# Attention scores as full-array fp32r matmuls on stacked key parts, and the turn of the older mix between the two score products

## The reference, cut to what matters

```python
def diff_attention(q, k, v, q_pos, k_pos, lam):
    s = jnp.einsum("bqhcd,bkhcd->bhcqk", q, k, preferred_element_type=jnp.float32) * (HEAD_DIM ** -0.5)
    mask = k_pos[None, :] <= q_pos[:, None]
    s = jnp.where(mask, s, NEG)
    p = jax.nn.softmax(s, axis=-1)
    w = p[:, :, 0] - lam * p[:, :, 1]
    return jnp.einsum("bhqk,bkhe->bqhe", w.astype(v.dtype), v)
```

## Time and profile before

| | us |
|---|---|
| median of three runs | 2425.14 |
| lowest and highest run | 2422.55, 2428.04 |
| span of the profiled execution | 2420.9 |
| PE busy in the span | 2349.3 (97%) |
| DVE, ACT and POOL busy | 1508.1, 750.4, 843.5 |

### The profile page before, as it was taken

One profiled execution on the slowest core, in us unless ns is written; L12 is line 12 of the kernel. 1 busy time (PEld: TensorE's weight loads), 2 busy tenths in 40 slices (PEclk: granted clock), 3 DMA queues, 4 the chain that ended last, 5 costly groups with the idle time before them and its releaser, 6 DMA issues.

```text
span 2420.9 us, 40635 instructions
## 1 busy us (share of the span) xinstructions
PE 2349.3 (97%) x16326; PEld 2276.2 (94%) x16326; DVE 1508.1 (62%) x2499; ACT 750.4 (31%) x1440; POOL 843.5 (35%) x557
## 2 busy tenths in 40 slices
PE   7899999999999999999999999999999999999998
PEld 6889999999999999999999766699999999999997
DVE  9993257555555576775534577756755555557766
ACT  4452134333333211031100377843433333320103
POOL 0003325544445443332332000043555444443431
PEclk9899999999999999999999999999999999999999
DMA  3155101222222422212256454210222222242212
GB/s 123 38 141 175 53 18 66 82 70 73 71 79 79 166 85 90 88 53 88 88 184 209 126 145 141 71 36 18 70 79 79 79 79 71 70 157 105 79 62 71
DMA packets 107540, 221.41 MB, mean 91 GB/s; under 512 B 35802, under 2 KB 59866, under 8 KB 107362
## 3 DMA queue, kind: packets, MB, share of 16 engines
q1 hardware_dynamic: 94130, 179.95, 23.3%
q10 hardware_dynamic: 13232, 38.94, 4.4%
HBM read 171.79 MB, written 44.71 MB: 89 GB/s over the span
## 4 chain that ended last, share of the span: by engine, by line
PE 84%; DVE 11%; issue 2%; ACT 1%; DMA 1%; POOL 0%; SPq 0%; DVEq 0%; ACTq 0%; POOLq 0%
PE pair L2130 45%; PE pair L2384 12%; PE pair L2387 12%; PE pair L2388 12%; PE pair L2617 1%; DVE nmx L1933 1%; DVE act_lo L1454 1%; DVE Vp L1373 1%; DMA zn<-zblk 1%; DVE wmix L2010 1%; DVE acc L1373 1%; DVE Vp L1795 1%; PE pair L2298 1%; DVE act_lo L1407 0%; DVE G_im L1373 0%
## 5 line engine op out<-in xcount | busy, mean ns | idle before, releaser
L2384 PE MATMUL pair<-act_hi,w_hi 128*128 128x344 f32 x1408 | 450.0, 320 | 6.7 <-DVE gate L1373 3.0
L2388 PE MATMUL pair<-act_hi,w_lo 128*128 128x344 f32 x1408 | 450.1, 320 | 0.0
L2387 PE MATMUL pair<-act_lo,w_hi 128*128 128x344 f32 x1408 | 449.9, 320 | 0.0
L2130 PE MATMUL pair<-act_hi,w_hi 128*128 128x344 f32 x1152 | 371.1, 322 | 2.7 <-DVE act_lo L1373 2.1
L2130 PE MATMUL pair<-act_hi,w_lo 128*128 128x344 f32 x1152 | 368.2, 320 | 0.0
L2130 PE MATMUL pair<-act_lo,w_hi 128*128 128x344 f32 x1152 | 368.0, 319 | 0.0
L732 POOL CAST w_hi<-w_raw 128x1024 fp32r<-128x1024 f32 x90 | 114.8, 1276 | 722.8 <-issue 309.5
L1373 DVE TENSOR_TENSOR X<-X,pair 128x344 f32<-128x344 f32 x528 | 252.9, 507 | 150.8 <-PE pair L2130 150.8
L2130 PE MATMUL pair<-hid_hi,w_hi 128*128 128x344 f32 x1056 | 338.2, 320 | 1.1 <-POOL w_lo L735 1.1
L2130 PE MATMUL pair<-hid_lo,w_hi 128*128 128x344 f32 x1056 | 338.5, 321 | 0.0
L2130 PE MATMUL pair<-hid_hi,w_lo 128*128 128x344 f32 x1056 | 338.0, 320 | 0.0
(11 more groups left out here) (308 smaller groups left out, 4199.7 us busy)
## 6 DMA issues: line engine op xcount, KB each, us to landing
w_raw<-w SPq DMA_DIRECT2D x180, 512.0 KB, 4.0
hid_raw<-hid SPq DMA_DIRECT2D x20, 1032.0 KB, 5.7
hid<-gate ACTq DMA_DIRECT2D x22, 516.0 KB, 2.7
hid<-gate_odd ACTq DMA_DIRECT2D x22, 516.0 KB, 2.6
kpg<-cache_k SPq DMA_DIRECT2D x16, 512.0 KB, 5.4
vpg<-cache_v SPq DMA_DIRECT2D x16, 512.0 KB, 7.0
qd<-qt SPq DMA_DIRECT2D x28, 256.0 KB, 5.4
ublk<-x_b SPq DMA_DIRECT2D x8, 576.0 KB, 8.3
```

Source lines behind the costliest of these rows:

```text
L2130: return t_.matmul(out, lhsT, rhs, start=start, stop=stop)
L2384: ins = t_.matmul(out, wh, rhs[k][0], start=first and k == 0, stop=False, skip_group_check=True)
L2387: t_.matmul(out, wh, rhs[k][1], start=False, stop=False, skip_group_check=True)
L2388: last = t_.matmul(out, wl, rhs[k][0], start=False, stop=k == HK - 1, skip_group_check=True)
```

## The change

It has six parts.

1. **Scores.** The key tile `kh` of a component has the high parts of its 64 dimensions on partitions 0 to 63 and the low parts on 64 to 127. The queries' high parts lie twice, in `qh`, and their low parts twice, in `ql0` or `ql1`. One component's scores are then two fp32r matmuls over 128 rows for each 512 columns or rest of them, high and low, and one mask matmul of 128 columns. Columns are in plain order; the maximum and the exponential read them so.
2. **Order on PE.** T(v-1) stands between S(v+1, 0) and S(v+1, 1), no longer behind both.
3. **Splitting 16 rows of queries and keys** in the projection stage: ACT copies 1024 columns into the high part (`high_of_rows`), POOL subtracts (`low_of_rows`), ACT stores both parts to the new HBM scratch `qk` (`store_split`). There are two high buffers and one low buffer, so each low row waits for the two stores of the row ahead of it. The store to `qt` is gone.
4. **Where POOL does it**: behind the weight split of pair 3 four rows, and behind those of pairs 4 to 9 two rows each. DVE's eviction into a slot of `stage` waits for the low row that is read from it.
5. **Loads of a head**: 13 transfers and 3.5 MB (4 of keys, 8 of queries, each 256 KB, and the values) in place of 9 and 2 MB. Those of head 1's keys move behind the last eviction of the projections.
6. Semaphores of `X` and of the last output are merged, and the scratch of POOL's descriptors is set to 1024 bytes.

```diff
+SPLIT_ORDER = (2, 3, 0, 1) + tuple(range(4, 2 * KT))
...
             def load_queries(h, par, into=None):
...
+                for c in range(2):
+                    for l, out in enumerate((high[:, 1 - c, :], low[1 - c])):
+                        for g in range(2):
+                            sp.dma_start(out[64 * g:64 * g + 64, :].bitcast(F32), d["qk"][0, l, 2 * h + c].rearrange("m j t -> (m j) t")
+                                         ).then_inc(hd_in[par], 16)
...
+            def low_of_rows(i):
+
+                pool.wait_ge(hl_hi, i + 1)
+                if i:
+                    pool.wait_ge(hl_out, 32 * i)
+                g.tensor_tensor(hq[:, 2, :], rows_in_turn(i), hq[:, i % 2, :].bitcast(F32), ALU.subtract).then_inc(hl_lo, 1)
...
+            for u in range(U_KVQ - 2, SEG1, 2):
+                split_one(u, 1)
+                split_one(u + 1, 1)
+                for i in {3: (0, 1, 2, 3), 4: (4, 5), 5: (6, 7), 6: (8, 9), 7: (10, 11), 8: (12, 13), 9: (14, 15)}.get((u - U_KVQ) // 2, ()):
+                    low_of_rows(i)
...
+            def store_split(i):
+
+                tt = SPLIT_ORDER[i]
+                act.wait_ge(hl_lo, i + 1)
+                for l, x in enumerate((i % 2, 2)):
+                    act.dma_start(rows_of(d["qk"][tt // KT, l])[tt % KT], hq[:, x, :].bitcast(F32)).then_inc(hl_out, 16)
+
+            def high_of_rows(i):
+
+                if i >= 2:
+                    act.wait_ge(hl_out, 32 * (i - 1))
+                a.activation(hq[:, i % 2, :], rows_in_turn(i), ACT.Copy).then_inc(hl_hi, 1)
+                if i:
+                    store_split(i - 1)
...
             def scores(v, x):
...
-                w = (i + 1) * 64
-                for g in range(2):
-                    rows = slice(64 * g, 64 * g + 64)
-                    mm(bank[2 * x + g][:, 0:w], (qd[par] if h else qd_first)[rows, x, i * P:(i + 1) * P], kh[rows, par, x, 0:w], True, False)
-                for g in range(2):
-                    rows = slice(64 * g, 64 * g + 64)
-                    last = mm(bank[2 * x + g][:, w - 64:w], identb[rows, :], maskb[rows, :], False, True)
-                last.then_inc(a_s, 1)
+                q = slice(i * P, (i + 1) * P)
+                high = (qh[par] if h else qh_first)[:, x, q]
+                low = ql1[x][:, q] if par else ql0[:, x, q]
+                for k0 in range(0, (i + 1) * P, SEQ // 2):
+                    ks = slice(k0, min(k0 + SEQ // 2, (i + 1) * P))
+                    final = ks.stop < (i + 1) * P
+                    mm(pair[x][:, ks], high, kh[par][:, x, ks], True, False)
+                    mm(pair[x][:, ks], low, kh[par][:, x, ks], False, final)
+                mm(pair[x][:, q], identb[:], maskb[:], False, True).then_inc(a_s, 1)
...
                 if v + 1 < NH * KT:
                     scores(v + 1, 0)
-                    scores(v + 1, 1)
                 if v >= 1:
                     turn(v - 1)
+                if v + 1 < NH * KT:
+                    scores(v + 1, 1)
```

More of the change, by code:

```diff
@@ L140, in build @@
         identb = place("identb", [P, P], BF16)
-        maskb = place("maskb", [P, 64], BF16)
+        maskb = place("maskb", [P, P], BF16)
         ones = place("ones", [P, P], F32)
@@ L158, in build @@
         ngain = place("ngain", [P, 2, KT], F32)
+        HQ_AT = top[0]
+        hq = place("hq", [P, 3, SEQ], F32R)
         STMP_AT = top[0]
@@ L317, in build @@
         blk_in = sem("blk_in")
-        x_in = [sem(f"x_in{n}") for n in range(NC)]
+        x_in = sem("x_in")
         w_in = [sem(f"w_in{r}") for r in range(4)]
@@ L1904, in _ @@
             c.step(v_.tensor_scalar(ngain[:], gains[:, 2:4, :], -1.0, None, ALU.mult))
-            for n in range(NC):
-                dve.wait_ge(x_in[n], 16)
+            dve.wait_ge(x_in, 16 * NC)
             with dve.Fori(0, KT - 2) as m:
@@ L1941, in _ @@
                     dve.wait_ge(d_smp, kvq_tile - 2)
+                    if kvq_tile - 3 < 2 * KT and not slots[kvq_tile - 3][1]:
+                        dve.wait_ge(hl_lo, SPLIT_ORDER.index(kvq_tile - 3) + 1)
                     for x in range(2):
@@ L1956, in _ @@
                 slot = slots[kvq_tile][0]
-                if not slots[kvq_tile][1]:
+                if kvq_tile >= KT and not slots[kvq_tile][1]:
                     seen[slot] += 16
@@ L2763, in constants @@
     tok = order[:P]
[L2764 to L2774 removed]
+    masked = np.where(tok[None, :] > tok[:, None], f(-1e30), f(0))
     nvec = np.concatenate([np.arange(NW), L * np.arange(NJ), L * NJ * np.arange(NI)]).astype(f)
```

114 lines of the change are left out of this document (56 added, 58 removed).

## The result

The changed kernel takes 2470.7 us (median of 4 runs, 2466.1 to 2474.4); the kernel before takes 2425.0. The ratio is 1.019, with a 95% interval of 1.0177 to 1.0203. The direction was forecast; the size was not: +45.7 us in place of +14.3, and outside the range of 2427 to 2453.

What follows compares the result with a forecast made beforehand. PE, busy 97% of the span, was taken as the bound. Attention +12.8 and projections +1.5 us gave +14.3 on the profiled span 2420.9, so 2435.2, or 2439.4 as a median; range 2427 to 2453.

Steps and rivals of the forecast that it cites:

- What bounds the kernel: Whole kernel: PE, busy 97% of the span; in attention it stops 36.8 us for exponentials, which the moved turn could fill.
- The scores themselves: small gain: Attention scores: same streaming rate, less fixed time; gain 0.6 us a head, with ends 0.7 and -0.6.
- the 0.23 of four passes: 128-column score matmuls: might fall back to four passes, 1.2 us a head, 9.6 in all; within a rival of chance 0.16.
- The rival of the doubled stream: Attention scores: leaving two row tiles doubles their stream, 61.6 us added, 2501 in all; chance 0.02.
- The turn between the scores: a loss: Attention: scores, maximum, exponential, W, turn and next scores form one ring across four engines; loss 2.2 us a head.
- from 3 blocks on the chain is shorter than PE's own work and the lag stays: Attention, steps after T(2): PE, by then 1.8 us late, falls no further behind.
- Splitting rows in the projections: nearly hidden: Projection stage: low rows 8.1 us apart stop PE ahead of pair 4; cost 1.5 us, with ends 0 and 5.
- the next pairs need 7.3 + 2.4 + 8.1 = 17.8 of POOL in 22.7 us of PE [...], so they recover: Projection stage, pairs after pair 4: POOL's work fits within PE's time for a pair, so the pairs recover.
- Loads: Attention heads: 9 MB more, 41 GB/s added to 106, costed at nothing; head 1 up to 3 us if cover fails.
- The sum: Whole kernel: +12.8 us in attention and +1.5 in the projections, +14.3 together.

Runs made afterwards that it cites:

- the first experiment: The changed kernel with the turn put back behind both components' scores, the new scores, splits and loads kept: 2437.8 us, ratio 1.0061 to the kernel before.

## Why the prediction was too small, point by point

**What bounds the kernel: right.** PE's stops were the right place to look, and both parts of the loss are stops of PE.

**"The scores themselves: small gain": right.** Forecast 0.6 us a head; with the old order, 29.37 - 28.38 = 1.0 in head 3, and 5.5 to 6.6 over the stage, 0.7 to 0.8 a head. The working was partly off: 8 blocks take 1.08 us, not 0.98, so the two steps with 8 and 7 blocks are 0.1 us longer each than before, and the gain lies in the steps with 5 blocks and fewer, about 0.2 each. Much of it is 0.17 us in which PE passed from O, on the full array, to scores on half of it, as the rows of the first experiment show. The starts of 512-column matmuls lie 0.23 apart, as forecast (0.31 behind the first of a component), those of 128 columns 0.06 to 0.14: not the 0.23 of four passes. The rival of the doubled stream is refuted: 8 blocks take 1.00 us on two 64-row tiles and 1.08 on the full array. That does not test the Trainium skill's rule on row tiles (TensorEngine Tiling (Array Packing), Overview), since the number format changed with the tiling; no run here has the same format on both.

**"The turn between the scores: a loss": the mechanism right, one term of it far too small.** Forecast 2.2 us a head; measured 31.95 - 28.38 = 3.6. Step by step in head 3, the changed kernel's times less those of the old order: 0.41 in the step behind T(7), where the prediction had 0.4; 1.88 in the step with T(1), where it had 1.7 (T(0) waits 0.99, not 0.77); then 0.55, 0.54 and 0.25 in the steps with T(2), T(3) and T(4), where it had 0.1 in all. So the step that failed is "from 3 blocks on the chain is shorter than PE's own work and the lag stays": 1.3 us a head in place of 0.1. T(2) and T(3) each wait 0.35 for `wT`, behind the exponential of the scores that the turn itself had put off. The kernel with the turn back in two steps and the one with it between in two others confirm the first two terms, 1.88 and 0.4.

**The clock: missing from the sum.** A stop of PE was priced at its length. Behind some stops the granted clock is at 1.2 GHz for 3.4 us, which costs up to 1.7 us more: four times in the attention stage and twice in the projections, 8 to 10 us of the 43. The rows show it behind T(1)'s wait of 2.07 us in one head, while the same wait in head 3 left the clock at 1.00; what decides between the two stays open. Head by head, 8 x (31.95 - 29.37) = 20.6 and four falls at 1.1 to 1.7 give 25.0 to 27.4, against 26.5 measured (the fall that the kernel before has lies behind its mark).

**"Splitting rows in the projections: nearly hidden": the step that failed most.** Its first half was right to 0.2 us: rows 8.3 apart, and the 1.5 us stop ahead of pair 4. The second half, "the next pairs need 7.3 + 2.4 + 8.1 = 17.8 of POOL in 22.7 us of PE [...], so they recover", counted POOL's time alone. Missing were what POOL's work does to VectorE's instructions (19.0 us for what took 15.2 and, at the wrong moment, 4 us of stop), ScalarE's queue, in which row 7's stores (issued at 1222.59) stood behind a wait for roped rows (14.97 us for POOL), and SyncE's queue, in which `qb` and the pages stand behind weight loads that POOL's splits release. The forecast was 1.5, the stage lost 14.3; with two low buffers and the turn back it lost 1.2. It was a failure to follow each queue that the change made longer.

**"Loads": right for the heads.** No stop for a head's loads is seen; in the attention stage the transfers rose from 106 to 144 GB/s without one.

**The sum.** Of 43.2 in the profiled executions, the forecast had 14.3. Of the 28.9 missing, the turn's size is 11 (8 x 1.4), the clock in attention some 6, the projections 13, the scores gave 3 back, and 2 are what lies ahead of and behind the two stages.

## What to carry to other kernels

Before an operation is put between two others to fill a wait, follow what it waits for back through all engines; if the chain comes back to an operation that the filler delays, it is a ring, and the walk has to go round until the times repeat, with the delays of each step fed into the next. Work given to an idle engine has three prices beside its own time: the queue behind it, the queues of those that wait for it, and, for GpSimd, the stretching of VectorE's operations beside it. A stop of PE is to be priced with the fall of the clock that may follow it.

## What the runs showed of the hardware

GpSimd work for which VectorE does not wait by the program nearly doubled the mean time of VectorE's two-input operations beside it (703 to 1292 ns): nine of 24 took 1.3 us or more, in place of two. The granted clock fell to the lower of its two levels, 1.2 GHz, for 3.4 us, in some runs 6.8, at or just behind stops of PE of 1.2 to 5 us, and stayed at 2.4 behind others of the same length: with waits of 2.07 us in the changed kernel both are seen. Scores on the full array with fp32r operands cost about the same as scores on two halves with fp32 ones (1.08 against 1.00 us for 8 blocks), and save the 0.17 us of passing between the two.
